# LayerNorms worked out in PSUM, each tile in two neighbouring banks, with two tiles transposed earlier

## The reference

```
layer 0: h = conv_sgu_mixer(x)             # projection to 2048; causal conv of width 31, gated spatial product; projection back
layer 1: h = dilated_attention_mixer(x)    # q, k, v of 3 groups x 8 heads x 128; merged; projection back
x = layer_norm(ALPHA * x + h,         ln_g[l, 0], ln_b[l, 0])          # ALPHA = 4 ** 0.25
x = layer_norm(ALPHA * x + swiglu(x), ln_g[l, 1], ln_b[l, 1])          # swiglu: hidden 2816

layer_norm(x, g, b): xc = x - mean(x);  xc * rsqrt(mean(xc * xc) + 1e-5) * g + b
```

## Time and profile before

| | |
|---|---|
| median of three runs | 1447.7 us |
| the profiled execution's own time | 1443.48 us |
| its span, first to last instruction | 1441.2 us |
| busy: TensorE / VectorE / ScalarE / GpSimd | 97% / 37% / 34% / 44% |
| chain that ended last | TensorE 84%, VectorE 10%, ScalarE 3% |
| mean granted clock of TensorE | 0.991 |
| DMA | 134.75 MB, mean 93 GB/s |
| stores of the output | 4 of 512 KB, 2.6 us to landing |

### The profile page before, as it was taken

How to read it: one execution, slowest core, us unless ns; L and a number is a source line. 1 busy time by engine, 2 the same in 40 slices (tenths; PEclk the granted TensorE clock), 3 DMA queues, 4 the chain that set the end, 5 groups by cost and what they waited for, 6 DMA issues and landing times.

```text
span 1441.2 us, 17188 instructions
## 1 busy us (share of the span) xinstructions
PE 1401.7 (97%) x6695; PEld 1189.8 (83%) x6695; DVE 527.1 (37%) x763; ACT 492.7 (34%) x741; POOL 638.9 (44%) x293
## 2 busy tenths in 40 slices
PE   7998999999999999999999999999999999999996
PEld 6875788888888878888898888899878888888885
DVE  4987611111140036666532665632161111110004
ACT  4464532322222243333323334333253222232123
POOL 5874544444344445333432333433254444444442
PEclk9999999999999999999999999999999999999998
DMA  9222233333422323232322322332123333243221
GB/s 282 77 86 73 59 107 98 102 88 101 133 93 97 102 59 88 74 88 88 105 86 73 88 78 69 89 117 87 54 63 104 87 102 101 88 131 103 88 73 59
DMA packets 175183, 134.75 MB, mean 93 GB/s; under 512 B 4198, under 2 KB 157562, under 8 KB 175129
## 3 DMA queue, kind: packets, MB, share of 16 engines
q1 hardware_dynamic: 175128, 133.98, 30.9%
HBM read 131.87 MB, written 2.10 MB: 93 GB/s over the span
## 4 chain that ended last, share of the span: by engine, by line
PE 84%; DVE 10%; ACT 3%; issue 1%; POOL 1%; DMA 0%; DVEq 0%; SPq 0%; POOLq 0%; ACTq 0%
PE pq L560 12%; PE pq L561 12%; PE pq L562 12%; PE ps L561 5%; PE ps L560 5%; PE ps L562 5%; DVE ps L1364 3%; PE ps L582 3%; PE ps L584 3%; PE ps L583 3%; PE pq L582 3%; PE pq L584 3%; PE pq L583 3%; PE pq L880 3%; PE pq L881 3%; PE pq L882 3%
## 5 line engine op out<-in xcount | busy, mean ns | idle before, releaser
L487 POOL TENSOR_TENSOR w_lo<-w_stage,w_hi 128x1024 fp32r<-128x1024 f32 x236 | 569.5, 2418 | 740.2 <-ACT w_hi L970 740.2
L560 PE MATMUL pq<-xt_hi,w_hi 128*128 128x512 f32 (+1 forms) x904 | 341.5, 378 | 9.7 <-DVE xt_lo L1262 5.7
L562 PE MATMUL pq<-xt_hi,w_lo 128*128 128x512 f32 (+1 forms) x904 | 338.4, 374 | 0.0
L561 PE MATMUL pq<-xt_lo,w_hi 128*128 128x512 f32 (+1 forms) x904 | 338.4, 374 | 0.0
L970 ACT ACTIVATE w_hi<-w_stage 128x1024 fp32r<-128x1024 f32 x236 | 246.1, 1054 | 255.0 <-PE ps L584 183.8
L560 PEld LDWEIGHTS pq<-xt_hi,w_hi 128*128 128x128 f32 x904 | 171.9, 190 | 40.2 <-DVE xt_lo L1262 7.5
L562 PEld LDWEIGHTS pq<-xt_hi,w_lo 128*128 128x128 f32 x904 | 172.1, 190 | 29.7
L561 PEld LDWEIGHTS pq<-xt_lo,w_hi 128*128 128x128 f32 x904 | 172.1, 190 | 29.0
L1526 DVE TENSOR_TENSOR hidden<-ps,hidden 128x512 f32<-128x512 f32 x44 | 30.4, 692 | 369.5 <-PE ps L562 369.5
L560 PE MATMUL ps<-xt_hi,w_hi 128*128 128x512 f32 (+1 forms) x368 | 140.3, 381 | 0.0
L561 PE MATMUL ps<-xt_lo,w_hi 128*128 128x512 f32 (+1 forms) x368 | 140.1, 381 | 0.0
(11 more groups left out here) (237 smaller groups left out, 1953.2 us busy)
## 6 DMA issues: line engine op xcount, KB each, us to landing
w_stage<-in_od_w_qkv_dram SPq DMA_DIRECT2D x72, 512.0 KB, 3.8
w_stage<-in_ffn_w_gate_dram SPq DMA_DIRECT2D x44, 512.0 KB, 3.8
w_stage<-in_ffn_w_up_dram SPq DMA_DIRECT2D x44, 512.0 KB, 3.9
w_stage<-in_ffn_w_down_dram SPq DMA_DIRECT2D x44, 512.0 KB, 3.4
w_stage<-in_ev_w_in_dram SPq DMA_DIRECT2D x16, 512.0 KB, 6.2
w_stage<-in_ev_w_out_dram SPq DMA_DIRECT2D x8, 512.0 KB, 3.3
w_stage<-in_od_w_out_dram SPq DMA_DIRECT2D x8, 512.0 KB, 3.4
x_res<-in_x_dram SPq DMA_DIRECT2D x4, 512.0 KB, 5.9
```

Of the source, the lines that this page charges most:

```text
L487: pool.tensor_tensor(w_lo[slab % RING][:, :], w_stage[slab % RING][:, :], w_hi[slab % RING][:, :].bitcast(F32), ALU.subtract).then_inc(w_l ...
L560: pe.matmul(ps[bank][:, at], hi[:, k, :], xt_hi[:, k, at], start=(k == 0), stop=False)
L561: pe.matmul(ps[bank][:, at], hi[:, k, :], xt_lo[:, k, at], start=False, stop=False)
L562: last = pe.matmul(ps[bank][:, at], lo[:, k, :], xt_hi[:, k, at], start=False, stop=(k == KD - 1))
```

## The change

- All eight banks are one tensor `pq`. Tile i of a row product is collected in `pq[2i]` and `pq[2i + 1]` (`tile_banks`), so one instruction can take both. `ps` keeps its numbers for all other uses and points at other banks.
- `norm_in` writes `ALPHA * x + product` back into the tile's two banks, with one instruction of 1024 and one sum. ScalarE squares from there. `norm_gain` now stands before the scale: `bank = (bank - mean) * norm_g`, one instruction of 1024, when the squares are done. `scale` reads the banks, multiplies by `rstd` and writes `x_res`; `shift` is gone. `add_shift` waits for the scale.
- Tiles 0 to 2 go this way in all norms, e = 3 too. Tile 3 ends with `norm_end` on VectorE, and its halves are stored by one transfer each.
- Tile 0 is transposed after the first of tile 3's three slabs, tile 1 after the second.
- VectorE multiplies tile 2 by the gain after the low parts of tiles 0 and 1 and before tile 3's sum. ScalarE splits slab 1 after the high part of tile 1. GpSimd subtracts slab 2 before it adds tile 2's offset.
- In the gating mixer the spatial products use the banks (5, 2, 0, 7) of `ps`, and so wait for the gelus that read those banks (`u_set`); the mean is in `ps[3]`, the variance in `ps[5]`; the tiles' order in the second half of the gating rows is 0, 2, 3, 1.

```diff
-        pq = ctx.enter_context(nc.psum_tensor("pq", [P, 4, 512], F32))
-        ps = [pq[:, j, :] for j in range(4)]
-        ps += [ctx.enter_context(nc.psum_tensor(f"ps{j}", [P, 512], F32)) for j in range(4, 8)]
+        pq = ctx.enter_context(nc.psum_tensor("pq", [P, 8, 512], F32))
+        ps = [pq[:, j, :] for j in (1, 2, 5, 6, 0, 3, 4, 7)]
...
+        pair_banks = (5, 2, 0, 7)
+        def halves(a):
+            return a.rearrange("p (a n) -> p a n", a=2)
+        def tile_banks(i):
+            return pq[:, 2 * i:2 * i + 2, :]
+        def turn_bank(e, i, half):
+            return ps[i + 2 + 2 * half] if e == 2 and i >= 2 else pq[:, 2 * i + half, :]
...
             def add_shift(e, i):
+                pool.wait_ge(x_scaled, e * SHIFT_TILES + i + 1)
                 for half in range(2):
-                    pool.wait_ge(x_gained, 2 * (e * SHIFT_TILES + i) + half + 1)
...
                     split_low(following + 1)
-                    add_shift(e, 2)
                     split_low(following + 2)
+                add_shift(e, 2)
+                if e < 3:
                     split_low(following + 3)
...
                 if c == 2:
                     pe.wait_ge(v_set, TILES)
+                    pe.wait_ge(u_set, 1)
                     spatial(0)
                     spatial(1)
-            pe.wait_ge(acc_set, 1)
+            pe.wait_ge(u_set, 3)
             spatial(2)
...
-                            if j == 1 and e < 3:
-                                turn_x(e + 1, 0)
+                            if j < 2 and e < 3:
+                                turn_x(e + 1, j)
...
-                if e < 3:
-                    turn_x(e + 1, 1)
...
                 def scale(i):
+                    act.wait_ge(x_gained, e * TILES + i + 1)
                     act.wait_ge(ln_scale, e * SHIFT_TILES + i + 1)
-                    act.activation(x_res[:, i, :], x_res[:, i, :], ACT.Identity, bias=shift[:, i:i + 1],
-                                   scale=rstd[:, i:i + 1]).then_inc(x_scaled, 1)
+                    act.activation(halves(x_res[:, i, :]), tile_banks(i), ACT.Copy, scale=rstd[:, i:i + 1]
+                                   ).then_inc(x_scaled, 1)
...
-                split(1)
                 high(0)
                 root(2)
                 high(1)
-                if e < 3:
-                    scale(2)
+                split(1)
+                scale(2)
                 split(2)
...
+                banks = tile_banks(i)
+                link.mark(dve.scalar_tensor_tensor(out=banks, in0=halves(x_res[:, i, :]), scalar=ALPHA, in1=banks,
+                                                   op0=ALU.mult, op1=ALU.add, accum_out=row_sum[:, i:i + 1]))
...
+            def norm_gain(e, i):
+                banks = tile_banks(i)
+                dve.wait_ge(ln_sq, e * TILES + i + 1)
+                dve.scalar_tensor_tensor(out=banks, in0=banks, scalar=neg_mean[:, i:i + 1], in1=halves(norm_g[:, :]),
+                                         op0=ALU.add, op1=ALU.mult).then_inc(x_gained, 1)
...
+            def norm_end(e, i):
+                dve.wait_ge(ln_std, e * TILES + i + 1)
+                link.mark(dve.reciprocal(rstd[:, i:i + 1], std[:, i:i + 1]))
+                link.wait()
+                dve.wait_ge(x_gained, e * TILES + i + 1)
+                for half in range(2):
+                    cols = slice(half * 512, (half + 1) * 512)
+                    dve.scalar_tensor_tensor(out=x_res[:, i, cols], in0=pq[:, 2 * i + half, :], scalar=rstd[:, i:i + 1],
+                                             in1=norm_b[:, cols], op0=ALU.mult, op1=ALU.add).then_inc(x_normed_end, 1)
             def norm(e):
...
                 norm_in(e, 0)
+                norm_gain(e, 0)
                 norm_scale(e, 0)
                 norm_in(e, 1)
+                norm_gain(e, 1)
                 norm_scale(e, 1)
                 norm_in(e, 2)
                 low(0)
+                low(1)
+                norm_gain(e, 2)
                 norm_scale(e, 2)
                 norm_in(e, 3)
+                norm_gain(e, 3)
+                norm_end(e, 3)
                 low(2)
                 low(3)
```

More of the change, by code:

```diff
@@ L466, in _ @@
             load_down(S_DOWN1, 1, 3)
[L467 to L471, removed]
-                sp.dma_start(out[0, i * P:(i + 1) * P, :], x_res[:, i, :]).then_inc(out_stored, 16)
-            sp.wait_ge(out_stored, 16 * TILES)
+            for i in range(SHIFT_TILES):
+                sp.wait_ge(x_normed, 2 * (3 * SHIFT_TILES + i + 1))
+                sp.dma_start(out[0, i * P:(i + 1) * P, :], x_res[:, i, :]).then_inc(out_stored, 16)
+            for half in range(2):
+                cols = slice(half * 512, (half + 1) * 512)
+                sp.wait_ge(x_normed_end, 2 * 3 + half + 1)
+                sp.dma_start(out[0, SHIFT_TILES * P:SEQ, cols], x_res[:, SHIFT_TILES, cols]).then_inc(out_stored, 16)
+            sp.wait_ge(out_stored, 16 * (TILES + 1))
         @block.gpsimd
@@ L588, in turn_x @@
                 for half in range(2):
-                    bank = ps[turn_banks(e, i)[half]]
+                    bank = turn_bank(e, i, half)
                     if e and i < SHIFT_TILES:
@@ L656, in _ @@
                     for k in range(2):
-                        last = tokens(slab, 512 * k, 512, v_banks[i], xt_hi[:, 2 * s + k, :], xt_lo[:, 2 * s + k, :],
+                        last = tokens(slab, 512 * k, 512, ps[v_banks[i]], xt_hi[:, 2 * s + k, :], xt_lo[:, 2 * s + k, :],
                                       i, s == 0 and k == 0, s == 3 and k == 1)
@@ L666, in spatial @@
                         half = (h % 2) * GROUP_CH
-                        last = pe.matmul(ps[4 + pair][half:half + GROUP_CH, n * P:(n + 1) * P],
+                        last = pe.matmul(ps[pair_banks[pair]][half:half + GROUP_CH, n * P:(n + 1) * P],
                                          v_tok[:, n, h * GROUP_CH:(h + 1) * GROUP_CH], wsp_t[:, h, :],
@@ L681, in _ @@
                     pe.wait_ge(v_set, TILES)
+                    pe.wait_ge(u_set, 1)
                     spatial(0)
                     spatial(1)
-            pe.wait_ge(acc_set, 1)
+            pe.wait_ge(u_set, 3)
             spatial(2)
-            pe.wait_ge(u_set, 1)
+            pe.wait_ge(u_set, 2)
             for c, (which, count) in enumerate(((chunk_summed, 1), (chunk_summed, 2), (acc_set, 1), (acc_set, 2))):
                 pe.wait_ge(which, count)
-                last = pe.matmul(ps[2][:, :], ones[:, :], acc[:, c, :], start=(c == 0), stop=(c == CC - 1))
+                last = pe.matmul(ps[3][:, :], ones[:, :], acc[:, c, :], start=(c == 0), stop=(c == CC - 1))
             last.then_inc(mean_done, 1)
@@ L700, in gating_rows @@
                         pe.wait_ge(mixlo_set, 2 * s + 2)
-                    for i in (1, 2, 3, 0) if half else range(TILES):
-                        if half == 0 and s == 0 and i == 2:
+                    for i in (0, 2, 3, 1) if half else range(TILES):
+                        if half == 0 and s == 0 and i == 3:
                             pe.wait_ge(xc_set, CC)
-                        if half and s == 0 and i == 0:
+                        if half and s == 0 and i == 1:
                             pe.wait_ge(std_set, 1)
@@ L707, in gating_rows @@
                             row = CC + 2 * s + k
-                            last = tokens(slab, 512 * k, 512, i + 4 * half, mix_hi[:, row, :], mix_lo[:, row, :],
+                            last = tokens(slab, 512 * k, 512, pq[:, 2 * i + half, :], mix_hi[:, row, :], mix_lo[:, row, :],
                                           i, s == 0 and k == 0, False)
@@ L712, in gating_rows @@
                             pe.wait_ge(sq_sum_set, 1)
-                            pe.matmul(ps[4][:, :], ones[:, :], acc[:, 0, :], start=True, stop=True
+                            pe.matmul(ps[5][:, :], ones[:, :], acc[:, 0, :], start=True, stop=True
                                       ).then_inc(var_done, 1)
@@ L719, in both_halves @@
                 for half in range(2):
-                    last = tokens(slab, 512 * half, 512, i + 4 * half, t_hi[:, row, :], t_lo[:, row, :], i, first, end)
+                    last = tokens(slab, 512 * half, 512, pq[:, 2 * i + half, :], t_hi[:, row, :], t_lo[:, row, :], i, first, end)
                 return last
```

71 lines of the change are left out of this document (18 added, 53 removed).

## The result

Five timed runs of the changed kernel gave 1433.8 to 1436.14 us, median 1435.01; the kernel before, beside them, 1443.09 to 1450.67, median 1444.27. The ratio is 0.9926, with a 95% interval of 0.991 to 0.9943: faster by 0.74%, 9.3 us by the medians.

What follows compares the result with a forecast made beforehand. The prediction took TensorE as the bound, busy 1401.7 us of a 1441.2 us span. Norms -7.0, clock +3.3, end -2.3 and mixer 0 summed to -6.0 us: 1441.5 us, range 1436 to 1448.

Steps and rivals of the forecast that it cites:

- The clock: TensorE's granted clock behind the new wait in the norms between stages: two falls in three norms, +3.3 us, bounds 0 and +4.9.
- split wait: Norms between stages: TensorE waits 1.5 and 0.8 us for the halves of tile 2, four transposes in the middle.
- The norms at full clock: Three norms between stages: transposes end 2.5 us earlier, 2.0 at e = 1; sum -7.0 us.
- 0.1 either way: Norms: margin on the squares from PSUM (1.15 us) and the scale (1.24 us), both taken as unchanged.
- The multiplication: VectorE's 1024 wide gain in the norms, tile banks as source and target: 1.3 us, between 1.2 and 1.5.
- The slower rival: Norms: operations reading and writing the same two banks take twice as long; +18.6 us, 1466; chance 0.06.
- The second rival: Norms: early transposes buy nothing, as GpSimd's new order meets slow operations; +0.6 us, 1448.3; chance 0.20.
- The end: Last norm (e = 3) and stores: tile 3 done -2.0 us, last transfer -0.3; sum -2.3 us.
- The store's -0.3: The end: last transfer has 256 KB, the other half 0.6 us ahead; -0.3 us, bounds 0 and -0.7.
- The mixer: Gating mixer: spatial products wait for the first gelu, +1.9 us of standing still, covered by a later wait; 0 us.
- The cover: Gating mixer: TensorE's 4.67 us wait for GpSimd's tap sums covers the later start; without it +1.9 us.
- the first rival: Norms: the clock doesn't fall after the split wait; -9.3 us, 1438.4; chance 0.27.

Runs made afterwards that it cites:

- experiment 10: The changed kernel with tile 3 stored by one transfer of 512 KB when both halves are done; 1434.91 us, ratio 0.9928 to the kernel before.
- experiment 7: The changed kernel with GpSimd subtracting a quarter of slab 2 once more ahead of tile 2's addition, each norm between stages; 1438.65 us, 0.9958 to the kernel before.
- experiment 3: The changed kernel's whole order, but norm work in x_res in SBUF, only the product read from the banks; 1444.99 us, 1.0002 to the kernel before.
- experiment 4: The change's bank layout and gating mixer alone, with norms, transposes and stores of the kernel before; 1444.94 us, 0.999 to the kernel before.
- experiment 1: The changed kernel with tiles 0 and 1 transposed late again, norm work still in PSUM; 1437.36 us, 0.9942 to the kernel before.
- experiment 5: The changed kernel, but GpSimd adds tile 2's offset before it subtracts slab 2; 1426.31 us, 0.9865 to the kernel before.
- experiment 6: Experiment 5 with ScalarE's split of slab 3 ahead of tile 2's high parts; 1426.85 us, 0.9875 to the kernel before.
- experiment 8: The changed kernel with GpSimd subtracting half of slab 2 once more ahead of tile 2's addition, each norm between stages; 1440.09 us, 0.997 to the kernel before.
- experiment 2: The kernel before with the two earlier transposes only, norms in SBUF as they were; 1456.42 us, 1.0075 to the kernel before.
- experiment 9: The changed kernel with GpSimd subtracting all of slab 2 once more ahead of tile 2's addition, each norm between stages; 1444.26 us, 0.9996 to the kernel before.

## Why the prediction was wrong, point by point

**The step that failed is "The clock": "I take two falls in three norms, +3.3 us".** It was put on a split wait of 1.5 and 0.8 us. The wait came out 1.12 and 0.57, and behind it the changed kernel's profile has no fall, that of experiment 10 one in three. With the wait at about its forecast size (1.9 and 0.56 in experiment 7, 1.5 and 1.0 in experiment 3) two of three came each time. So the rate fits, as far as three norms of a profile can show a rate, and the size of the wait was wrong. It was wrong because tile 2 was added sooner: its first half was ready at 175.34 for a forecast 175.9, while TensorE ended its half columns at 174.2 for 174.4. That is the next term. One fall of 1.7 us came at a place that I had not named, the scores of the attention. Clock in the sum: +1.7 instead of +3.3.

**The norms at full clock: -7.0 forecast, -8.6 measured** (3.07 twice and 2.5 for the middle one, its fall taken out). This term missed by as much as the clock's, 1.6 us. The path was as worked out: tile 0 without a wait, tile 1 with 0.2 (0.6 forecast), half columns with none, then GpSimd's order as the new last wait. Most of each 0.6 us came from short operations that I had left unchanged: the scale is 1.118 for 1.244 before, squares 1.118 for 1.152, the mean's small operation 0.15 for 0.21. On the way to tile 2 lie two scales, two squares and two of the small operations, by these rows 0.4 us, an estimate; the rest was not traced. Only 0.034 of the scale's 0.126 is the place of the numbers, since in SBUF the new scale takes 1.152 (experiment 3); the rest came with its new form (Copy, without `shift`). It is the side on which I had put "0.1 either way". At e = 1 slab 3 was waited for as forecast, 0.37 us where the sum had 0.5. The Trainium skill, "Perfetto Trace Analysis", section "Optimizing Scalar/DVE Operations", names the side for ScalarE (93 ns on SBUF, 51 on PSUM), and the squares agree: 34 ns less. For VectorE the 65 ns more that the prediction estimated from it do not show: an end's half is 0.746 from PSUM, 0.744 was the best from SBUF.

**The multiplication** was priced 1.3, measured 1.293; the sum of 1024 took 1.211; the addition 1.285. The slower rival (a bank read and written by one instruction costs double) is refuted by that row alone. The second rival (slow operations under GpSimd) did not come about, but experiment 3 shows such a time for the same order in SBUF, 0.2 us above the kernel before; there the multiplications were slow (2.282), and the additions mostly not (1.289 at the median).

**The end: -2.3 forecast, -1.9 measured**, in parts that differ. The forecast's round of a tile, "2.85 + 1.3 + 0.2 = 4.2", is a slip, the sum is 4.35. Measured it is 4.0 (the sums of tiles 2 and 3 start at 1418.96 and 1422.97), less than TensorE's 4.09, so VectorE does not fall behind. Tile 3's sum starts 0.2 us behind TensorE's end rather than 0.7 (1422.97 against 1410.53 + 12.27 = 1422.80), and the last store is issued at 1428.53, 2.6 us nearer to TensorE's end than before (8.3 became 5.7); -2.0 was forecast. But from there to the last instruction it takes 3.7 us, not 3.0. That the small transfer waits for the one in front of it is a guess that no run shows by itself. The store's -0.3 is refuted by experiment 10.

**The mixer: 0 forecast**, 0.15 us less measured; experiment 4 gives a ratio with 1 in its interval. The cover was there, though the wait for the taps became 1.09 and not the 2.8 that was left by the working: see experiment 4.

**The time itself.** Span 1441.2 to 1432.2 is -8.6 + 1.7 - 1.9 - 0.15 = -9.0. I had set my -6.0 against a median of 1447.7 from three runs. Five runs gave 1444.27, near the profiled 1443.48; 3.4 us of the miss in the absolute time is that. In differences the result is the first rival's (-9.3), and its condition, no fall behind the norms, is what the profile shows. That its number fits is luck: its -7.0 was 1.6 us too small and its -2.3 was 0.4 too large, and it had no fall of 1.7 us elsewhere.

Left open: why the clock fell behind the 2.26 us wait of L831 in seven of the profiles (the changed kernel's and experiments 1, 5, 6, 7, 8, 10) and not in the other five, and why the same wait of 1.7 us in a norm was followed by a fall once. No kernel here changes only that. How often the unprofiled runs fell at each place is not known either.

## What to carry to other kernels

Where VectorE and GpSimd work at the same time, count the SBUF sources of VectorE's operations: giving one of two sources a place in PSUM took away waits of up to 1.1 us per operation, and here, with the new order in place, that was worth the whole gain. When a wait is removed, look in the other engines' order lists for the one that is late next, and try swapping it: one line in GpSimd's list was worth another 5.8 us by the profiles, 8.7 by the medians. Look up where in time a wait stands before aiming at it: a total by line put the 0.8 us of experiment 6 into a norm. And set a forecast difference against the profiled execution's own time, not against a median of three runs.

## What the runs showed of the hardware that was not expected

- An early TensorE made the kernel slower by 11.5 us without any added work (experiment 2), through one GpSimd operation that moved 1.3 us forward onto a VectorE operation with two SBUF sources: a pair of 512 wide operations took 5.41 us, 1.4 undisturbed.
- A tiny VectorE operation is held as well: the kernel before makes `shift` from two SBUF columns of 128x1 in 0.16 us at best and 1.43 at worst. At 168.48 it takes 1.42, beside GpSimd's subtraction (167.54 to 169.88) and right ahead of the low parts that TensorE's 2.87 us wait for the earlier trace rows. The change leaves it out.
- The clock after a wait is not a function of the wait. In the norms, by the sum of the wait's one or two pieces: behind 1.7 us it fell in one of nine (the changed kernel, experiments 1 and 10), behind 2.5 to 2.7 us in seven of nine (experiments 3, 7 and 8), behind 2.9 us and more in all twelve (the kernel before, experiments 2, 4, 9). Elsewhere, behind one whole wait: 2.0 us for the gelu, five of ten profiles; 2.3 us for the scores, seven of twelve; 2.9 us for `mix_lo`, one of five.
- A fall costs less when waits lie inside it: 1.0 and 1.4 us instead of 1.6 in experiment 9.
